# Up projection by groups of 512 columns in two sets of four banks

## The reference

```python
h = rms_norm(x, ffn_norm)
u = h @ w_up                                   # 2048 -> 2 * 5632
u = sum(conv_w[j] * up[:, j:j + S] for j in range(3)) + conv_b   # up: u shifted by two tokens
a, b = split(u, 2)                             # 5632 each
x = x + (silu(a) * b) @ w_down                 # 5632 -> 2048
```

## Time and profile before

| | |
|---|---|
| time, median of 3 runs | 1080.38 us (1080.21 to 1080.58) |
| profiled execution | 1080.29 us |
| its span, first to last instruction | 1078.6 us |
| TensorE busy | 1073.7 us |
| VectorE busy | 908.6 us |
| ScalarE busy | 633.9 us |
| up projection | about 365 to 857 us of the span |
| down projection | about 857 to 1075 us |

### The profile page before, as it was taken

How to read it: one execution, slowest core, us unless ns; L and a number is a source line. 1 busy time by engine, 2 the same in 40 slices (tenths; PEclk the granted TensorE clock), 3 DMA queues, 4 the chain that set the end, 5 groups by cost and what they waited for, 6 DMA issues and landing times.

```text
span 1078.6 us, 18188 instructions
## 1 busy us (share of the span) xinstructions
PE 1073.7 (100%) x6543; PEld 928.9 (86%) x6543; DVE 908.6 (84%) x1376; ACT 633.9 (59%) x930; POOL 79.8 (7%) x114
## 2 busy tenths in 40 slices
PE   9999999999999999999999999999999999999998
PEld 9888888888888889888888988888888888888887
DVE  7878988889655678888888888888877889999997
ACT  7677676757554655545555555545555566656663
POOL 4500000000000000000000000000000000000000
PEclk9999999999999999999999999999999999999999
DMA  8656687777889888798888888889888789798884
GB/s 275 183 163 176 190 229 223 216 223 222 234 258 245 278 236 235 240 256 239 249 232 243 237 255 245 227 258 247 271 240 235 218 282 319 256 309 315 260 289 163
DMA packets 192336, 260.77 MB, mean 242 GB/s; under 512 B 9605, under 2 KB 143894, under 8 KB 192022
## 3 DMA queue, kind: packets, MB, share of 16 engines
q1 hardware_dynamic: 176246, 216.24, 62.4%
q0 software_dynamic: 13344, 38.80, 17.6%
q10 hardware_dynamic: 2688, 5.00, 1.2%
HBM read 255.02 MB, written 43.78 MB: 277 GB/s over the span
## 4 chain that ended last, share of the span: by engine, by line
PE 99%; DMA 1%; DVE 0%; SPq 0%; issue 0%; DVEq 0%
PE bank L1821 38%; PE bank L1829 20%; PE bank L2216 7%; PE bank L2215 7%; PE bank L2214 7%; PE bank L2067 3%; PE bank L1868 3%; PE bank L2068 3%; PE bank L2069 3%; PE bank L1869 3%; PE bank L1870 3%; PE bank L1789 1%; PE bank L1897 1%; DMA xt<-in_x_dram 1%; PE bank L2106 0%; PE bank L1986 0%
## 5 line engine op out<-in xcount | busy, mean ns | idle before, releaser
L792 ACT CAST w_hi<-raw 128x1024 fp32r<-128x1024 f32 x299 | 311.9, 1048 | 252.7 <-PE bank L1829 118.4
L1201 DVE TENSOR_TENSOR w_lo<-raw,w_hi 128x1024 fp32r<-128x1024 f32 x299 | 363.8, 1222 | 108.1 <-ACT w_hi L792 107.5
L1821 PE MATMUL bank<-hs,w_hi 128*128 128x512 f32 x1792 | 423.0, 391 | 0.0
L1821 PEld LDWEIGHTS bank<-hs,w_hi 128*128 128x128 f32 x1792 | 331.3, 188 | 66.2 <-issue 0.9
L1829 PEld LDWEIGHTS bank<-hs,w_lo 128*128 128x128 f32 x1792 | 224.6, 192 | 5.7 <-issue 0.2
L1829 PE MATMUL bank<-hs,w_lo 128*128 128x256 f32 x1792 | 227.3, 283 | 0.0
L1171 ACT CAST hi_slot<-slot 128x1024 fp32r<-128x1024 f32 (+1 forms) x102 | 117.7, 1187 | 64.7 <-DVE slot L1746 25.2
L1728 DVE TENSOR_TENSOR slot_lo<-slot,hi_slot 128x1024 fp32r<-128x1024 f32 (+1 forms) x102 | 136.7, 1388 | 5.8 <-ACT hi_slot L1171 4.7
L2216 PE MATMUL bank<-hi_slot,gated 128*128 128x512 f32 (+1 forms) x194 | 75.1, 387 | 0.0
L2214 PE MATMUL bank<-hi_slot,gated 128*128 128x512 f32 (+1 forms) x194 | 75.1, 387 | 0.0
L1646 DVE SCALAR_TENSOR_TENSOR C<-U,cols,C 128x256 f32<-128x256 f32 x176 | 73.3, 478 | 0.0
(11 more groups left out here) (248 smaller groups left out, 1183.8 us busy)
## 6 DMA issues: line engine op xcount, KB each, us to landing
raw<-in_w_ffn_up_dram SPq DMA_DIRECT2D x176, 512.0 KB, 5.2
u_sums<-in_w_ffn_down_dram POOLq DMA_DIRECT2D x58, 512.0 KB, 6.7
raw<-in_w_in_dram SPq DMA_DIRECT2D x51, 512.0 KB, 4.5
slot<-in_w_ffn_down_dram SPq DMA_DIRECT2D x38, 512.0 KB, 5.0
slot<-u_sums SPq DMA_DIRECT2D x74, 256.0 KB, 5.6
raw<-in_w_in_dram SPq DMA_DIRECT2D x66, 256.0 KB, 4.2
raw<-in_w_out_dram SPq DMA_DIRECT2D x32, 512.0 KB, 5.7
u_sums<-u_sums POOLq DMA_DIRECT2D x16, 512.0 KB, 7.4
```

Of the source, the lines that this page charges most:

```text
L792: act.copy(w_hi[:, i, :], raw[:, i, :]).then_inc(units_hi, 1)
L1201: dve.tensor_tensor(w_lo[:, i, :], raw[:, i, :], w_hi[:, i, :].bitcast(F32), ALU.subtract)\
L1821: m = pe.matmul(banks[b][:, :], w_hi[:, i, c], hs[:, 4 * i + k, :], start=(first and k == 0), stop=(final and k == 3))
```

## The change

Up works on groups of 512 columns. A unit is two k-tiles by 512 columns (rows of 2 KB in DRAM instead of 1 KB); a quad covers eight k-tiles of 512 columns, and two quads (halves) make up a group's a or b. Four banks are in use at a time: 2, 3, 6, 7 for a and 0, 1, 4, 5 for b. The number and the shapes of matmuls stay. The works keep their size of 256 columns, so two a works come behind the two a quads and two b works behind the two b quads: a of g, a of g + 1, b of g, b of g + 1. `C` gets a third tile, since two results of a must be kept until b comes. Work w waits for the end of its pair of quads and converts quad w + 3; the units of the third quad are converted ahead of the first work. The first park of sums stands behind the second b work of its pair, the second behind the following a work. ScalarE's and VectorE's loops are written out; TensorE's loop has 10 turns of four quads. The down projection's first pass gathers its sums in 2, 3, 6, 7, with waits on evacuations and on the gated products for its first quadruples.

```diff
-        C = sb_at(place, "C", [P, 2, 2, SEQ])
+        C = sb_at(place, "C", [P, 3, 2, SEQ])
+        banks_up = [[(bank[2], bank[3]), (bank[6], bank[7])], [(bank[0], bank[1]), (bank[4], bank[5])]]
+        banks_row = [bank[6], bank[0]]
-        sums_of = [[bank[4], bank[5], bank[6], bank[7]], [bank[0], bank[1], bank[2], bank[3]]]
+        sums_of = [[bank[2], bank[3], bank[6], bank[7]], [bank[0], bank[1], bank[4], bank[5]]]
 # SyncE
-            with sp.Fori(0, UP_GROUPS) as g:
-                load_channels(g * 2 + Q_UP, w_up_v, g * GC)
-                load_channels(g * 2 + Q_UP + 1, w_up_v, g * GC + D_FF)
+            with sp.Fori(0, UP_PAIRS) as n:
+                for ab in range(2):
+                    for half in range(2):
+                        for i in range(RING):
+                            load_unit(n * 4 + Q_UP + 2 * ab + half, i, w_up_v, 8 * half + 2 * i, 2, n * GT + ab * D_FF, GT)
 # ScalarE
+            for i in range(RING):
+                make_hi(Q_UP + 2, i)
...
+            def a_work(g, work):
+                quad = work + Q_UP + 3
+                some_hi(quad, [0])
+                if g > 1:
+                    act.wait_ge(ab_made, g - 1 + FREE)
+                last_tap(work, 2 * (g % 2), 0, g)
+                some_hi(quad, [1])
+                act.wait_ge(tap0, work * 2 + 2)
+                a = C[:, 2 * (g % 2), :, :].rearrange("p c t -> p (c t)")
                 act.activation(a, a, ACT.Silu).then_inc(silu_a, 1)
+                some_hi(quad, [2, 3])
+            def b_work(g, work):
+                quad = work + Q_UP + 3
+                some_hi(quad, [0])
+                last_tap(work, 1, 1, g)
+                some_hi(quad, [1, 2])
                 act.wait_ge(ab_made, g + 1 + FREE)
+                act.copy(gated[:, g * 2:g * 2 + 2, 0:SEQ], C[:, 1, :, :]).then_inc(gated_hi, 1)
+                some_hi(quad, [3])
...
+            for n in range(UP_PAIRS):
+                for g in (2 * n, 2 * n + 1):
+                    a_work(g, 2 * n + g)
+                    if g - 1 in range(RESIDENT_SUMS, SEVENS) and g % 2 == 0:
+                        park_sums(g - 1)
+                for g in (2 * n, 2 * n + 1):
+                    if g == UP_GROUPS - 1:
+                        act.wait_ge(sum_parked, 16 * PARKED_SUMS)
+                    b_work(g, 2 * n + g + 2)
+                    if g - 1 in range(RESIDENT_SUMS, SEVENS) and g % 2 == 1:
+                        park_sums(g - 1)
+                    if g < SEVENS:
+                        hi_of_sums(g)
 # VectorE
+            def some_lo(quad, units):
+                for i in units:
+                    if quad < Q_DOWN + 2:
+                        make_lo(quad, i)
...
-                evacuate(G_UP + ab, n, (n + Q_UP + 1) * RING, dst)
+                evacuate(banks_up[ab][g % 2], work, (Q_UP + 2 * (work // 2) + 2) * RING, dst)
...
+            for n in range(UP_PAIRS):
+                for g in (2 * n, 2 * n + 1):
+                    a_work(g, 2 * n + g)
+                for g in (2 * n, 2 * n + 1):
+                    b_work(g, 2 * n + g + 2)
+                    if g < SEVENS:
+                        lo_of_sums(g)
 # TensorE
+            def high_wide(half, i, banks):
+                for k in range(2):
+                    for f in range(4):
+                        c = slice(k * GT + f * P, k * GT + (f + 1) * P)
+                        m = pe.matmul(banks[f // 2][f % 2][:, :], w_hi[:, i, c], hs[:, 8 * half + 2 * i + k, :],
+                                      start=(half == 0 and i == 0 and k == 0), stop=(half == 1 and i == 3 and k == 1))
+                return m
...
+            for half in range(2):
+                for i in range(RING):
+                    pe.wait_ge(h_lo, (CHUNKS + 2 * half + i // 2 + 1) * TT)
+                    first_wide(half, i, banks_up[0], turn_last if half == 0 and i == 1 else None)
+                    if half == 1 and i == 0:
+                        pe.wait_ge(groups_evacuated, G_UP + 2)
+                        spread_rms(1)
+            pe.wait_ge(row_made, 2)
+            for half in range(2):
+                quad_wide(Q_UP + 2 + half, half, banks_up[1])
+            with pe.Fori(1, UP_PAIRS) as n:
                 for ab in range(2):
-                    pe.wait_ge(groups_evacuated, g * 2 + ab + G_UP + 1)
-                    quad_channels(g * 2 + ab + Q_UP, pair_of(G_UP + ab))
+                    pe.wait_ge(groups_evacuated, n * 4 + 2 * ab + G_UP)
+                    for half in range(2):
+                        quad_wide(n * 4 + 2 * ab + half + Q_UP, half, banks_up[ab])
...
+                    if pair == 0 and at == 0:
+                        pe.wait_ge(groups_evacuated, G_DOWN + BANK_PAIRS - 2)
+                    if pair == 0 and at < OLD_RING:
+                        pe.wait_ge(gated_lo, K_PAIR_AT[pair][at] + 1)
```

More of the change, by code:

```diff
@@ L1634, in _, with taps @@
                 make_lo(Q_UP + 1, i)
+            for i in range(RING):
+                make_lo(Q_UP + 2, i)
             dve.wait_ge(row_made, 2)
-            def taps(n, ab, g, quad):
+            def some_lo(quad, units):
+                for i in units:
+                    if quad < Q_DOWN + 2:
+                        make_lo(quad, i)
+            def taps(work, c_tile, ab, g, quad):
                 dst = U[:, :, 2:SEQ + 2]
-                evacuate(G_UP + ab, n, (n + Q_UP + 1) * RING, dst)
-                make_lo(quad, 0)
+                evacuate(banks_up[ab][g % 2], work, (Q_UP + 2 * (work // 2) + 2) * RING, dst)
+                some_lo(quad, [0])
                 for tap, before, after in ((1, tap2, tap1), (0, tap1, tap0)):
@@ L1648, in taps, with a_work @@
                                                  ALU.mult, ALU.add).then_inc(after, 1)
[L1649 to L1657, removed]
+                some_lo(quad, [1])
+            def a_work(g, work):
+                taps(work, 2 * (g % 2), 0, g, work + Q_UP + 3)
+                some_lo(work + Q_UP + 3, [2, 3])
@@ L1844, in unit_channels, with low_wide, first_wide, quad_wide @@
                 last.then_inc(units_used, 1)
-            def quad_channels(quad, banks):
+            def high_wide(half, i, banks):
[5 more added lines that the diff above has]
+                return m
+            def low_wide(half, i, banks):
+                for k in range(2):
+                    for f in range(4):
+                        c = slice(k * GT + f * P, k * GT + (f + 1) * P)
+                        m = pe.matmul(banks[f // 2][f % 2][:, 0:SEQ], w_lo[:, i, c], hs[:, 8 * half + 2 * i + k, 0:SEQ],
+                                      start=False, stop=False)
+                return m
+            def first_wide(half, i, banks, in_the_middle=None):
+                pe.wait_ge(units_split, (Q_UP + half) * RING + i + 1 + RING)
+                if i % 2 == 0:
+                    high_wide(half, i, banks)
+                    last = low_wide(half, i, banks)
+                else:
+                    low_wide(half, i, banks)
+                    if in_the_middle is not None:
+                        in_the_middle()
+                    last = high_wide(half, i, banks)
+                last.then_inc(units_used, 1)
+            def quad_wide(quad, half, banks):
                 for i in (0, 1):
                     pe.wait_ge(units_split, quad * RING + i + 1 + RING)
-                    high(i, banks, i == 0, False)
+                    high_wide(half, i, banks)
                 for i in (0, 1):
-                    low(i, banks).then_inc(units_used, 1)
+                    low_wide(half, i, banks).then_inc(units_used, 1)
                 for i in (2, 3):
                     pe.wait_ge(units_split, quad * RING + i + 1 + RING)
-                    low(i, banks)
+                    low_wide(half, i, banks)
                 for i in (2, 3):
-                    high(i, banks, False, i == RING - 1).then_inc(units_used, 1)
+                    high_wide(half, i, banks).then_inc(units_used, 1)
             def unit_tokens(quad, i, group, src, k0, k_all):
@@ L1954, in spread_rms @@
                 for t in range(TT):
[L1955 removed]
+                    last = transpose(banks_row[n][:, t * P:(t + 1) * P], ss[:, t:t + 1].broadcast_to([P, P]))
                 last.then_inc(row_spread, 1)
```

92 lines of the change are left out of this document (26 added, 66 removed).

## The result

| | before | after |
|---|---|---|
| time, median | 1080.35 us | 1083.84 us |
| profiled execution | 1080.29 us | 1083.56 us |
| its span | 1078.6 us | 1081.8 us |

The changed kernel is slower: the ratio is 1.0037, with an interval of 1.0024 to 1.0050. The forecast of 1083.9 us and its range held. The difference of the medians is 3.5 us, that of the two profiled executions 3.27 us; the traces explain the second.

What follows compares the result with a forecast made beforehand. TensorE was taken to set the time, with VectorE next, first in down. A 6.8 us delay less 2.0 idle and 1.15 lead left 3.6 us; 1080.29 + 3.6 = 1083.9 us, range 1080.0 to 1086.5 us.

Steps and rivals of the forecast that it cites:

- The end of up: Behind the last up quad: open exchanges in b of g = 21 start VectorE's first seven about 6.8 us later, at 877.3 us.
- What hides of it: From 870.52 to 912.62 us, first to eighth seven: 2.0 us of VectorE idle time and 1.15 us of lead absorb delay.
- The stall: Start of down: TensorE waits 3.6 us in small steps, from the first seven's second piece to the eighth's; chance 0.68.
- faster matmuls: Rival, all 44 up quads: four banks or a longer-held moving tile shorten the pace, say 1077 us; chance 0.07.
- The longer loop: Rival, TensorE's up loop: 9 returns fetching instructions cost 13.5 us, 1097 us with the stall; chance 0.08, shared with another up stall.
- The loads: Up weights: 2 KB runs instead of 1 KB may land faster than 5.2 us, but gain nothing since no matmul waits.
- Covered: Rival, start of down: VectorE's late start is smaller or regained, giving 1080.4 to 1082.4 us; chance 0.17.
- The parking: In up: sums of g = 14 park later, ScalarE awaits the 5.1 us landing before rounding g = 15; cost taken as 0.
- the wait near 735 us: Sign that the prediction is wrong: TensorE waits in up near 735 us because of the parked sum.

## Why the prediction was right

**The end of up.** It was built from exchanges that lie open. The estimate was 6.8 us and a first seven at 877.3 us; measured are 6.94 us against the start of down, and 877.30 us. VectorE's evacuation at 870.36, ScalarE's taps at 872.46 and its rounding of the product at 875.69 us stand where the steps put them. The rows of before that carried this are those at 869.38 and 870.52 us: the last conversion stands directly ahead of the first seven, so that no conversion is left for a second b work.

**What hides of it.** 2.0 us of idle time and 1.15 us of lead were forecast, 3.15 in all. The experiments give 3.0 us, three times (3.41, 3.93 and 6.41 us lost of 6.40, 6.94 and 9.40). From below, 2.78 us cost nothing. The two parts were each a little off, in opposite ways. From the first seven's subtraction to the eighth's VectorE takes 40.34 us before (870.52 to 910.86) and 38.12 us in the changed kernel (877.30 to 915.42), so 2.2 us of idle time went. That leaves 0.8 us of lead and not 1.15. The forecast read the waiting matmul's start from the chain, at 913.77 us; TensorE's timeline has it at 913.60. A held-up matmul also starts 0.05 us behind the subtraction's end (917.23 against 915.42 + 1.76 us), and the next start is 0.11 us late.

**The stall.** 3.6 us were forecast, in small steps from 880 to 917 us; measured are 3.9 us from the first to the last matmul of down, at six places from 879.9 to 916.6 us and none later. The difference is the two terms above: 0.14 us more delay and 0.15 us less cover.

**What was not foreseen.** The two ends of the span take 0.16 and about 0.5 us off, and cancel the 0.3 us by which the stall was undersized. That is luck: the forecast of the total was nearer than its terms. The earlier start is not the change's: down starts at 857.16 us before and at 857.10 and 856.97 us in the old kernel with four and nine multiplications, and from 856.97 to 857.44 us in the changed kernels that lose nothing at 758 us, so it varies from profile to profile. The shorter tail stands in every kernel of the table with the changed order (3.16 or 3.17 us), and in none with the old one (3.64 to 3.66 us): the last stores land 1.9 us after their issue in place of 2.5. Why they do was not tried.

**What was taken as nothing.** The chain of TensorE in mid-up, in the changed kernel:

```profile
497.88 7.28 PE bank L1871 x32
505.16 3.83 PE bank L1879 x32
```

A quad is 7.28 + 3.83 = 11.11 us, with four banks as with two, so *faster matmuls* falls. *The longer loop* falls too: the instruction queue moved 33 packets in place of 31, where nine returns that each had to fetch would have added at least nine, and the windows show no idle time of TensorE in up. The packets are those of all engines together. The loads land in 4.8 us in place of 5.2 and gain nothing, as no matmul waited for them. *Covered* was a rival of size alone; the added multiplications show its limit at a delay of 3.0 us, where the prediction set it at 3.15.

**The parking** was held at nothing with a margin of about 0.1 us (second low part at 12.8, wanted at 12.9 us) for a landing in 5.1 us. That holds: at 3.94 us (in the changed kernel with added multiplications) and 4.25 us nothing, at 5.57 and 5.59 us 0.4 us. Of the 0.4 us 0.11 is the late second start, so the edge lies near a landing of 5.3 us, where the forecast had 5.2. But the landing varies from run to run, and the forecast's sum has one value for it. It also looked for the wait near 735 us; the park of g = 14 goes out at 746 us in the changed kernel, and the wait stands near 758 us.

## What to carry to other kernels

A coarser grouping moves no work, but it moves the moment at which the last results are free, and so how many works are left when the next stage starts; count those at the boundary, with the exchanges between engines that nothing covers any more. The price of such a delay is the delay less the smallest lead that the next stage's tight engine has further on, idle time up to there included, and idle work put in at the boundary of the old kernel measures that cover directly, without making the change. It holds for a delay of that engine alone: where weights came later too, the kernel lost 0.3 us more than the law says. Putting the remaining conversions between the exchanges got all of the loss back that the medians can show.

## What the runs showed of the hardware

- After a stall the second start is late too. In all six stalls of the changed kernel it came 0.335 to 0.338 us after the first, in place of 0.227, and 0.335 to 0.341 us in the old kernel with nine multiplications. A short stall therefore cost 0.11 us on top of its wait, 0.7 of the 3.7 us.
- A subtraction of 128 x 512 took GpSimd 1.56 us and VectorE 0.69 us, and VectorE's next subtraction (128 x 1024), which lay beside it for its first 0.65 us, took 1.74 in place of 1.22 us; that was seen once. The first one on GpSimd lengthened neither the subtraction of 128 x 1024 that VectorE had begun 0.83 us ahead of it (1.22 us) nor the two reductions of 128 x 512 that ran beside it (0.69 and 0.68 us).
- The same park of 384 KB, issued at the same point of the program, landed in 3.94, 4.25, 5.57 and 5.59 us in four kernels.
